# Hybrid decoder trunk on one core: each expert weight row stored as two halves of 4,096 bytes, 512 KB apart

## Chip, cores and metric

One core of a Trainium2 chip runs the kernel. The metric is the device time of one execution in microseconds, as the median of several runs. One more execution was profiled; all rows of the trace come from that one.

## What is computed

Two layers over 256 tokens of width 1024, all in float32. Each layer has a norm modulated by a conditioning vector, three parallel token mixers (a convolution module, a state-space module, an attention module), their gated merge, and then a feed-forward part. In layer 0 that is one dense SwiGLU of width 2816; in layer 1 it is eight experts of width 3584, of which each token uses two:

```python
def _swiglu(h, wg, wu, wd):
    return (jax.nn.silu(h @ wg) * (h @ wu)) @ wd

def _moe(h, router_w, router_b, wg, wu, wd):
    logits = (h @ router_w + router_b).astype(jnp.float32)
    top_v, top_i = lax.top_k(logits, MOE_TOPK)
    ...
    for e in range(N_EXPERTS):
        out = out + gates[..., e:e + 1] * _swiglu(h, wg[e], wu[e], wd[e])
    return out
```

A final norm follows. The weights of all eight experts are read in full: 8 x 3 x 1024 x 3584 values, 352 MB of the 531 MB that the kernel reads.

## The kernel before

**Work and stages.** Every large weight is cut on the host into units of 1 MB, stored so that one unit is a contiguous block of 128 rows (one for each partition of SBUF) of 2,048 float32 values, 8,192 bytes. The kernel goes through the stages in order: conditioning products, the input projection of layer 0, its mixers, its merge and its dense feed-forward part, then the same for layer 1 with the router and the experts at the end. Until the experts, SP loads units into a ring of six slots (L461 to L465), and POOL loads the units of the conditioning matrix (L544).

**The experts.** An expert has 42 units (`UNITS`, L48): for each of seven column groups of its hidden width two units of the gate matrix, two of the up matrix and two of the down matrix (`expert_units`, L83). They go in this order through 14 slots (`EXP_SLOTS`, L49; `eslot`, L180), which are pieces of several tensors: `aring`, `extra`, `ring`, `proj`, `xc`, `misc` and `sq`. So loads of `in_moe_units` stand in the trace under all these names. Unit u of an expert goes into slot u % 14.

**Who waits for whom.** `expert_load` (L467) is the one place that loads them; each load raises the semaphore `efull` of its slot by 16. PE waits for it in `arrived` (in `expert`), multiplies with the unit, and raises `unit_s` once for each unit that it is done with. SP runs a loop over the experts (L491 to L498): before it loads a unit it waits until the unit 14 places earlier is done with (L494, L497), so at most 14 units are ahead of PE. The first 14 loads of the first expert (L472 to L486) wait for the slots' earlier users, the last expert has a loop of its own (L500). Then SP stores the output in four DMAs of 128 rows of 2,048 bytes (L505 to L508); the destination's rows are 4,096 bytes apart.

**Order and sizes.** The experts are taken in an order that is found at run time (`turn`), and the matmuls of each are chosen by its number of tokens, rounded up to one of six sizes (`SIZES`, L46). For 32 tokens (`quarter_rows`, whose lines are L1046, L1065 and L1076) PE is done with a unit fastest. L984 and L1019 are the gate and up products and the down products where tokens are stationary, L1108 and L1124 those of large experts. At the end of each expert `prepare` turns a matrix (L1154) and gathers the next expert's tokens (L939). Each size is its own block of code, to which PE jumps at a change of expert (`expert_loop`, L421).

**On the host** `kernel` (L1974) puts the units of the experts together with `moe_layout` (L1938), in the shape expert, unit, row, 2048 (L1986).

Of the kernel before, what the change touches and what calls it, by code (L numbers as in the profile page):

```python
# [17 lines left out]
P = 128  # L18
# [12 lines left out]
FFN_DENSE, FFN_EXPERT, EXPERTS = 2816, 3584, 8  # L31
# [16 lines left out]
UNITS = 6 * GE  # L48
EXP_SLOTS = 14  # L49
# [44 lines left out]
def trunk(nc, x_cols, c_cols, par_cols, ada_units, dense_units, moe_units, out):  # L94
    fp32, i32 = mybir.dt.float32, mybir.dt.int32
    ALU, ACT, AX = mybir.AluOpType, mybir.ActivationFunctionType, mybir.AxisListType
    ds = bass.ds
# [4 lines left out]
    with ctx:  # L102
# [49 lines left out]
        for name, n in COLUMNS:  # L152
# [27 lines left out]
        eslot = ([aring[:, i, :] for i in range(ADA_SLOTS)] + [extra[:, :]]  # L180
                 + [ring[:, i, :] for i in range(SLOTS)]
                 + [proj[:, 48:56, :].rearrange("p a n -> p (a n)"), proj[:, 56:64, :].rearrange("p a n -> p (a n)"),
                    xc[:, 0:8, :].rearrange("p a n -> p (a n)"), misc[:, :], sq[:, :, :].rearrange("p a n -> p (a n)")])
# [155 lines left out]
        def released(key):  # L339

            kind, l, a = key
            if kind == "w":
                return proj_s, W_CHUNKS * l + a + 1
            if kind == "conf":
                return om_s, 16 * l + 2 * a + 2
            if kind == "attn":
                return om_s, 16 * l + 4 + 2 * a + 2
            if kind == "ssm":
                return om_s, 16 * l + 8 + a + 1
            if kind == "mix":  # L350
                return om_s, 16 * l + 12 + a + 1
            if kind in "gu":
                return gu_s, 2 * a + 2
            return dn_s, DN0 + a + 1
# [99 lines left out]
        @block.sync  # L454
        def _(sp):
            for i, a in enumerate(ADA_ORDER):
                sp.dma_start(ada_first[i], ada_units[a]).then_inc(afirst[i], 16)
                if i == 1:
                    sp.dma_start(xT[:, :, :], x_cols.rearrange("p (k n) -> p k n", k=KT)).then_inc(x_in_s, 16)

            for i, key in enumerate(ORDER):  # L461
                slot, _, before = PLAN[key]
                if before is not None:
                    sp.wait_ge(*released(before))
                sp.dma_start(ring[:, slot, :], dense_units[i]).then_inc(full[slot], 16)  # L465

            def expert_load(expert, u):  # L467

                sp.dma_start(eslot[u % EXP_SLOTS], moe_units[ds(expert, 1), u].rearrange("e p n -> p (e n)")  # L469
                             ).then_inc(efull[u % EXP_SLOTS], 16)  # L470

            for u in range(EXP_SLOTS):  # L472
                if u < ADA_SLOTS:
                    sp.wait_ge(apool_s, DEPTH * ADA_CHUNKS - ADA_FIRST)
                elif 3 <= u < 3 + SLOTS:
                    sp.wait_ge(*released(LAST[u - 3]))
                elif u in (9, 10):
                    sp.wait_ge(mg_s, 16 + 12)
                elif u == 11:
                    sp.wait_ge(gn_s, DEPTH)  # L480
                elif u == 12:
                    sp.wait_ge(om_s, 16 + 4)
                    sp.wait_ge(pv_s, HEADS_A * DEPTH)
                elif u == 13:
                    sp.wait_ge(h_s, 4 * KT)
                expert_load(0, u)  # L486
            def expert_of(place):
                return sp.value_load(turn[0:1, place], min_val=0, max_val=EXPERTS - 1)

            sp.wait_ge(ord_s, 1)  # L490
            with sp.Fori(0, EXPERTS - 1) as e:  # L491
                now, following = expert_of(ds(e, 1)), expert_of(ds(e + 1, 1))
                for u in range(EXP_SLOTS, UNITS):
                    sp.wait_ge(unit_s, e * UNITS + (u - EXP_SLOTS + 1))  # L494
                    expert_load(now, u)
                for u in range(EXP_SLOTS):
                    sp.wait_ge(unit_s, e * UNITS + (UNITS + u - EXP_SLOTS + 1))  # L497
                    expert_load(following, u)  # L498
            final = expert_of(slice(EXPERTS - 1, EXPERTS))
            for u in range(EXP_SLOTS, UNITS):  # L500
                sp.wait_ge(unit_s, (EXPERTS - 1) * UNITS + u - EXP_SLOTS + 1)
                expert_load(final, u)


            for q in range(2 * TT):  # L505
                sp.wait_ge(o_s, q + 1)
                t, cols = q % 2, slice((q // 2) * 512, (q // 2 + 1) * 512)
                sp.dma_start(out[0, t * P:(t + 1) * P, cols], o_tm[:, t, cols]).then_inc(od_s, 16)  # L508
            sp.wait_ge(od_s, 16 * 2 * TT)
# [1488 lines left out]
```

## Time and profile before

| | |
|---|---|
| median of 3 runs | 2032.22 us (2031.87 to 2032.5) |
| the profiled execution's own time | 2033.62 us |
| its span, first to last instruction | 2031.9 us |
| mean granted TensorE clock | 0.955 of full speed |
| PE busy (matmul / weight load) | 1887.1 us (93%) / 1326.6 us (65%) |
| DVE, ACT, POOL busy | 512.2, 279.6, 351.9 us |
| read from HBM | 531.08 MB, 262 GB/s over the span |
| expert loads | 336, of 1,024 KB each |

The profile shows one execution. Busy times are sums over the span, and a matmul's end is modelled, so a busy PE isn't PE at its peak. PE is matmuls and PEld weight loads; SPq is the queue in which SP issues DMAs. "DMA share" is the mean busy share of 16 DMA engines; the records of neighbouring packets overlap a little, so that it can be 1.01 or 1.02. The chain is the work that ended last, followed back from the end at each step to what released it. "issue" is time in which the engine waited for nothing that the profile shows.

### The profile page before, as it was taken

Reading aid. Unit: us, or ns where it says so; the run is one execution under the profiler, and the core shown is the slowest. Engines: PE = TensorE matmul, PEld = TensorE weight load, DVE = VectorE, ACT = ScalarE, POOL = GpSimd, SP = SyncE. Lnnn points to the kernel's source line nnn. Section 1 sums busy time; section 2 is a strip of 40 time slices with the busy share of each in tenths; the row PEclk is TensorE's granted clock in tenths of the full one; section 3 lists DMA queues with packets and bytes.
Section 4 is the critical chain, followed back from the end, with each engine's and each line's share of the span. In section 5 each row is a group of like instructions: output and inputs, shape, how many; then the busy total and the mean of one; then the engine's idle time right before and its main releaser. Section 6 shows DMA issues by size and latency. Waiting matters only on the chain.

```text
span 2031.9 us, 27702 instructions
## 1 busy us (share of the span) xinstructions
PE 1887.1 (93%) x11037; PEld 1326.6 (65%) x11038; DVE 512.2 (25%) x1144; ACT 279.6 (14%) x517; POOL 351.9 (17%) x215
## 2 busy tenths in 40 slices
PE   7999799989999999999977899998899979989796
PEld 5888588867776788888852688743444435555443
DVE  1794734110001292424141100011100110001112
ACT  2204212010000302422020000010000100010002
POOL 2609900079994000000000000000000000000000
PEclk8999899989999999999979899998999979999898
DMA  9645533257673444333459965589988899979993
GB/s 382 251 163 213 181 125 125 78 216 285 249 273 136 153 161 147 104 113 116 168 220 421 418 261 214 226 338 421 420 333 295 348 420 420 410 305 422 419 420 145
DMA packets 73857, 534.06 MB, mean 263 GB/s; under 512 B 8320, under 2 KB 8320, under 8 KB 8960
## 3 DMA queue, kind: packets, MB, share of 16 engines
q1 hardware_dynamic: 67680, 489.72, 61.6%
q0 software_dynamic: 5760, 41.95, 5.7%
q8 instruction: 103, 1.69, 0.3%
q10 hardware_dynamic: 288, 0.50, 0.1%
q14 instruction: 26, 0.21, 0.0%
HBM read 531.08 MB, written 1.05 MB: 262 GB/s over the span
## 4 chain that ended last, share of the span: by engine, by line
PE 83%; DMA 6%; DVE 4%; issue 3%; SPq 2%; ACT 2%; POOL 1%; DVEq 0%; ACTq 0%
PE ps L641 21%; PE ps L984 13%; PE ps L704 8%; PE ps L713 7%; PE ps L1019 6%; PE ps L1108 6%; PE ps L724 4%; PE ps L1124 3%; DMA xc<-in_moe_units 3%; DMA ring<-in_moe_units 3%; PE ps L1046 2%; PE ps L939 2%; SPq L469 2%; PE ps L1065 1%; PE ps L1076 1%
## 5 line engine op out<-in xcount | busy, mean ns | idle before, releaser
L641 PE MATMUL ps<-hT,ring 128*128 128x256 f32 x2048 | 455.4, 383 | 5.0 <-ACT hT L1236 5.0
L641 PEld LDWEIGHTS ps<-hT,ring 128*128 128x128 f32 x2048 | 390.6, 192 | 62.3 <-issue 8.3
L560 POOL TENSOR_TENSOR aring<-aring,ccol 128x2048 f32<-128x2048 f32 x40 | 145.0, 3624 | 234.5 <-ACT hT L1236 160.7
L713 PE MATMUL ps<-hT,ring 128*128 128x256 f32 x704 | 158.8, 388 | 4.0 <-ACT hT L1236 4.0
L713 PEld LDWEIGHTS ps<-hT,ring 128*128 128x128 f32 x704 | 136.5, 195 | 23.5 <-issue 4.4
L566 POOL TENSOR_TENSOR aring<-aring 128x1024 f32<-128x1024 f32 x80 | 149.5, 1869 | 6.3
L984 PE MATMUL ps<-ring,proj 128*64 128x256 f32 (+2 forms) x1144 | 131.2, 361 | 1.3 <-DMA ring<-in_moe_units 1.3
L1824 DVE TENSOR_TENSOR proj<-proj,ps 128x256 f32<-128x256 f32 (+2 forms) x28 | 14.6, 521 | 401.3 <-PE ps L984 401.3
L984 PEld LDWEIGHTS ps<-ring,proj 128*64 128x64 f32 (+2 forms) x1144 | 74.5, 132 | 52.4 <-issue 31.8
L1590 DVE SCALAR_TENSOR_TENSOR misc<-cpad,par,misc 128x256 f32<-128x256 f32 x240 | 102.7, 508 | 0.0
L704 PE MATMUL ps<-proj,ring 128*128 128x256 f32 x384 | 83.4, 379 | 0.0
L1241 ACT ACTIVATE proj<-ps 128x512 f32<-128x512 f32 x64 | 38.2, 596 | 328.5 <-PE ps L641 328.5
L704 PEld LDWEIGHTS ps<-proj,ring 128*128 128x128 f32 x384 | 72.8, 190 | 9.9
L724 PE MATMUL ps<-ring,proj 128*128 128x512 f32 x176 | 77.3, 592 | 0.0
L984 PE MATMUL ps<-aring,proj 128*64 128x256 f32 (+2 forms) x352 | 49.7, 420 | 27.8 <-issue 27.8
L1359 ACT ACTIVATE proj<-ps 128x256 f32<-128x256 f32 (+2 forms) x28 | 13.0, 464 | 380.9 <-PE ps L984 380.9
L1703 DVE TENSOR_TENSOR proj<-proj,ps 128x256 f32<-128x256 f32 x22 | 9.3, 421 | 211.9 <-ACT proj L1339 211.9
L1065 PEld LDWEIGHTS ps<-stk,proj 128*128 128x128 f32 x336 | 46.7, 222 | 23.7 <-issue 23.7
L984 PEld LDWEIGHTS ps<-aring,proj 128*64 128x64 f32 (+2 forms) x352 | 27.2, 154 | 51.9 <-issue 48.3
L1108 PE MATMUL ps<-proj,ring 128*128 128x160 f32 x416 | 60.0, 300 | 0.0
L704 PE MATMUL ps<-hT,ring 128*128 128x256 f32 x256 | 55.8, 380 | 3.0 <-DVE hT L1667 3.0
L1108 PEld LDWEIGHTS ps<-proj,ring 128*128 128x128 f32 x416 | 57.5, 190 | 0.8 <-issue 0.8
(345 smaller groups left out, 2117.7 us busy)
## 6 DMA issues: line engine op xcount, KB each, us to landing
ring<-in_moe_units SPq DMA_DIRECT2D x144, 1024.0 KB, 15.7
ring<-in_dense_units SPq DMA_DIRECT2D x121, 1024.0 KB, 5.0
aring<-in_moe_units SPq DMA_DIRECT2D x48, 1024.0 KB, 13.5
proj<-in_moe_units SPq DMA_DIRECT2D x48, 1024.0 KB, 18.1
aring<-in_ada_units POOLq DMA_DIRECT2D x40, 1024.0 KB, 6.0
extra<-in_moe_units SPq DMA_DIRECT2D x24, 1024.0 KB, 13.6
xc<-in_moe_units SPq DMA_DIRECT2D x24, 1024.0 KB, 20.1
misc<-in_moe_units SPq DMA_DIRECT2D x24, 1024.0 KB, 19.8
```

The source lines that it names most:

```text
L560: last = g.tensor_tensor(w, w, ccol[:, :].unsqueeze(2).broadcast_to([P, KT, 256]), ALU.mult)
L566: last = g.tensor_tensor(dst, w[:, 0:half_k, :], w[:, half_k:2 * half_k, :], ALU.add)
L641: last = mm(ps[:, n % 2, j * SEQ:(j + 1) * SEQ], wide(s)[:, k, j * P:(j + 1) * P], hT[:, k, :], start=(k == 0), stop=(k == KT - 1))
L704: last = mm(ps[:, idx % 2, j * SEQ:(j + 1) * SEQ], view(s)[:, k, (cols + j) * P:(cols + j + 1) * P], rhs[:, k, :], start=(k == 0), stop=(k ...
L713: last = mm(ps[:, j, c0:c0 + n], wide(w)[:, k, j * P:(j + 1) * P], x_src[:, k, 0:n], start=(k == 0), stop=(k == KT - 1))
L724: last = mm(dst, hm[:, b, j, t * P:t * P + rows], rows2(slot)[:, j, hf * 512:(hf + 1) * 512], start=(first and j == 0), stop=(stop and j = ...
L984: last = mm(ps[rows * c:rows * (c + 1), bank, 4 * t0:4 * (t0 + rows)], xg[:, 4 * h + k, t0:t0 + rows], w[:, k, 4 * rows * c:4 * rows * (c ...
L1019: last = mm(dst, hmt[:, g % 2, h0:h0 + rows], w[:, i, cols], start=(g == 0 and j == 0), stop=(g == GE - 1 and j == 3))
L1065: last = mm(ps[:, 4 + g % 2, c0 + j * n:c0 + (j + 1) * n], part[:, g % 2, j * P:(j + 1) * P], stk[:, :], start=True, stop=True)
L1108: last = mm(ps[:, j % 2, c0:c0 + n], w[:, k, j * P:(j + 1) * P], xg[:, 4 * h + k, 0:n], start=(h == 0 and k == 0), stop=(h == 1 and k == 3))
L1124: last = mm(dst, hmx[:, g % 2, j, t0:t0 + rows], w[:, i, cols], start=(g == 0 and j == 0), stop=(g == GE - 1 and j == 3))
L1590: v.scalar_tensor_tensor(cacc[:, m, :], cpad[:, m, ds(k, SEQ)], cwcol[:, l, ds(k * CT + m, 1)], cacc[:, m, :], ALU.mult, ALU.add).then_inc ...
```

## The change

Each unit of the experts is stored as two blocks of 128 rows of 1,024 values (4,096 bytes): the first halves of all rows, 512 KB, then the second halves. The load reads, for each partition, one piece from each block, and writes them side by side into the slot, so that the slot holds the same values at the same places. Each load then has 256 pieces of 4,096 bytes in place of 128 of 8,192. Number, order, size and waits of the loads are the same, and so are all other instructions.

```diff
             def expert_load(expert, u):
 
-                sp.dma_start(eslot[u % EXP_SLOTS], moe_units[ds(expert, 1), u].rearrange("e p n -> p (e n)")
+                sp.dma_start(eslot[u % EXP_SLOTS].rearrange("p (h n) -> p h n", h=2),
+                             moe_units[ds(expert, 1), u].rearrange("e h p n -> p (e h) n")
                              ).then_inc(efull[u % EXP_SLOTS], 16)
...
     t["moe_units"] = np.stack(moe_layout(inputs["moe_w_gate"][0], inputs["moe_w_up"][0], inputs["moe_w_down"][0])
-                              ).reshape(EXPERTS, UNITS, P, 2048)
+                              ).reshape(EXPERTS, UNITS, P, 2, 1024).swapaxes(2, 3)
```

## Rows read from the trace of the kernel before

**Rows 1.** The page: span, GB/s in 40 slices, chain by engine.

```profile
span 2031.9 us, 27702 instructions
...
GB/s 382 251 163 213 181 125 125 78 216 285 249 273 136 153 161 147 104 113 116 168 220 421 418 261 214 226 338 421 420 333 295 348 420 420 410 305 422 419 420 145
...
PE 83%; DMA 6%; DVE 4%; issue 3%; SPq 2%; ACT 2%; POOL 1%; DVEq 0%; ACTq 0%
```

**Rows 2.** The chain in order of time, expert stage: start us, us, what.

```profile
1092.60 26.79 DMA ring<-in_moe_units
...
1148.00 38.07 PE ps L1108 x256
...
1195.97 17.58 PE ps L1108 x128
...
1390.68 26.82 DMA xc<-in_moe_units
...
1625.08 26.85 DMA ring<-in_moe_units
...
1966.27 27.43 DMA xc<-in_moe_units
```

**Rows 3.** Busy time by windows of the expert stage; the first line names the columns.

```profile
core 0: us, PE busy (x) PEld busy (x) DVE busy (x) ACT busy (x) POOL busy (x), PEclk, DMA share, GB/s
1060.00:1070.00 10.00, 7.12 (x36) 4.39 (x36) 2.50 (x7) 1.35 (x2) 0.00 (x0) 0.66 0.80 318
1070.00:1120.00 50.00, 38.64 (x298) 14.02 (x300) 7.35 (x17) 3.50 (x8) 0.00 (x0) 0.93 1.01 421
...
1350.00:1420.00 70.00, 61.71 (x437) 28.13 (x430) 10.44 (x21) 7.14 (x15) 0.00 (x0) 0.90 1.01 421
...
1600.00:1660.00 60.00, 49.95 (x336) 20.74 (x339) 8.12 (x18) 4.37 (x10) 0.00 (x0) 0.85 1.01 422
...
1800.00:1810.00 10.00, 8.60 (x69) 4.22 (x68) 2.88 (x10) 1.31 (x3) 0.00 (x0) 1.00 0.64 242
1810.00:1820.00 10.00, 5.41 (x26) 3.15 (x28) 0.00 (x0) 2.65 (x5) 0.00 (x0) 0.66 0.36 117
...
1900.00:1990.00 90.00, 77.43 (x566) 41.00 (x564) 7.16 (x18) 6.82 (x15) 0.00 (x0) 0.92 1.01 420
...
2028.40:2030.90 2.50, 0.00 (x0) 0.00 (x0) 0.00 (x0) 0.40 (x1) 0.00 (x0) 1.00 1.03 385
```

**Rows 4.** Timeline of PE and PEld: start, us, instruction, in brackets idle before and releaser.

```profile
1129.37 0.14 PEld L1076 LDWEIGHTS ps<-xc,proj 128*32 128x32 f32 x4 [0.91 <-DMA xc<-in_moe_units]
...
1981.42 1.95 PE L984 MATMUL ps<-ring,proj 128*64 128x256 f32 x16 [0.63 <-DMA ring<-in_moe_units]
...
1993.74 0.20 PEld L1019 LDWEIGHTS ps<-xc,proj 128*64 128x64 f32 x4 [1.31 <-DMA xc<-in_moe_units]
```

**Rows 5.** The page: all DMA packets, and SP's queue (packets, MB, share of 16 engines).

```profile
DMA packets 73857, 534.06 MB, mean 263 GB/s; under 512 B 8320, under 2 KB 8320, under 8 KB 8960
...
q1 hardware_dynamic: 67680, 489.72, 61.6%
```

**Rows 6.** DMA queues in windows: q1 in 1070 to 1110, q10 in 13 to 18.

```profile
q1 hardware_dynamic: 2314, 16.79, 100.8%
...
q10 hardware_dynamic: 144, 0.49, 24.6%
```

**Rows 7.** SP's DMA instructions: expert loads into extra (ns min/median/max), and the output stores.

```profile
L469 SPq DMA_DIRECT2D extra<-in_moe_units x24: 332/333/1947, 979.8 to 1948.5; - x24
...
2027.38 1.82 SPq L508 DMA_DIRECT2D out<-proj  x4
```

**Rows 8.** Timeline of PE, first matmuls of an expert, with the idle time before.

```profile
1148.00 2.23 PE L1108 MATMUL ps<-proj,aring 128*128 128x160 f32 x7 [5.65 <-issue]
...
1814.59 1.98 PE L984 MATMUL ps<-aring,proj 128*64 128x256 f32 x8 [6.00 <-issue]
...
1913.76 6.15 PE L984 MATMUL ps<-aring,proj 128*64 128x256 f32 x32 [10.78 <-issue]
```

## Prediction

> **What bounds the kernel now.** I read the page first: the 40 slices show the DMA engines moving about 420 GB/s in several groups of slices of the second half, and mostly far below that before it [rows 1]. The first half can't be touched by a change of the expert loads alone; the question is what those groups cost. The shares of the chain say little (PE 83%, DMA 6%), since they are a mean over stages [rows 1]. So I followed the chain in order of time through the expert stage. It goes through a landing of expert weights four times: landings at 1119.4, 1417.5, 1651.95 and 1993.7, each 27 us after its issue [rows 2]. Between these the chain is PE alone. The experts differ in size: the first, third and fifth (32 token columns) use a unit faster than it can be loaded, the second and fourth are slow on PE and let the loads run 14 units ahead again. Rows by windows give the length of each full stretch [rows 3]:
>
> - A: the queue fills at about 1062 (share 0.80 in 1060 to 1070) and is full until the last wait on the chain at 1119.4: 57 us
> - B: 1350 to 1417.5: 67 us
> - C: 1600 to 1652: 52 us
> - D: after the loads had caught up (shares 0.64 and 0.36 in 1800 to 1820), from about 1830 to 1993.7: 164 us
>
> Together 340 us, all at 420 to 422 GB/s. The waits at the end of D are real though small: 0.63 us for one unit at 1981.4, and 1.31 before the weight load at 1993.74 [rows 4], so nothing of a later landing is hidden there. In A a wait of 0.91 us is seen as late as 1129.4 [rows 4], so A could count as 67 us rather than 57, and C likewise as 62; I keep that for the range (360 us).
>
> **What the change does to the packets.** The page has 73,857 packets, 67,680 on SP's queue; 466 loads and 4 stores make that 144 each, 128 rows and 16 completion packets [rows 5]. The 336 expert loads get 128 more each: 336 x 128 = 43,008, so 116,865 packets, with the same 531 MB. No instruction is added to an engine; SP issues as many DMAs as before, and the first 14 loads (before 1060) come while the DMA engines have idle time, so they cost nothing (the cover is PE's work to 1050).
>
> **The price of a packet.** Two stretches of the trace have the DMA engines full with packets of one size: expert loads of 8,192 bytes at 421 GB/s, and the output stores of 2,048 bytes at 385 GB/s [rows 3]. For one of 16 engines that is 8192 x 16 / 421 = 311.3 ns and 2048 x 16 / 385 = 85.1 ns a packet. The line through both has 0.0368 ns a byte and 9.7 ns for each packet. Eight more packets per engine and load would be 8 x 9.7 = 78 ns; as a part of the 9.7 ns (an eighth of a completion packet) is not doubled, I take 70 ns. A load goes from 1.0486 MB / 421 = 2.491 us to 2.56, 2.8% more, at about 410 GB/s.
>
> The bounds. Above: loads from 3,840-byte rows took 24.6% of 16 x 5 us = 19.7 us for 128 rows and 16 completions, so at most 154 ns a row, where 8,192 bytes took 100.8% of 640 us over 2,314 packets, of which 264 are completions, so at most 315 ns [rows 6]. A row of 4,096 would be 154 + 256 x 0.0368 = 163.4 ns, two of them 326.8, 12 ns over 315: 94 ns a load, 3.8%. Below: nothing, if the fixed part of a packet is hidden behind the data of the one before, and the stores' lower rate is due to their being stores. Not below nothing: no row has a rate above 422 GB/s. I take 70, since it comes from spacing and not from the length of records, which overlap (they sum to a share of 1.01). The Trainium skill (DMA: Bandwidth & Descriptors, section iDMA fabric) has one SP load stream of 1 MiB per DMA with 4 KiB rows at 408.7 GB/s; by that the load would take 2.566 us, an extra 75 ns, and the sum below 10.2 us. No run here shows that figure yet.
>
> **Sum.** 340 us / 2.491 = 136 loads on the path, 136 x 0.070 = 9.6 us: A 1.6, B 1.9, C 1.5, D 4.6. The terms add up: where a stretch ends in a wait, all that PE does later moves by its term, and the next full stretch starts later by as much. Between C and D the loads fall behind by 80 x 0.07 = 5.6 us from 1600 to 1800, of which PE's own shift takes 1.5; the 10 us in which the DMA engines stood idle between 1800 and 1820 cover the other 4.1 [rows 3]. If that cover were gone, D would begin at 1600.
>
> Against the profiled execution (2033.6 us, span 2031.9) this gives 2043.2. The median of the runs is 2032.2, so 1.4 lower: **2041.8 us**, 0.5% slower.
>
> **SP and its queue.** An expert load that finds room is issued in 0.33 us, the median; in the full stretches SP is often held for about 1.9 us or more, the most for this slot 1.95 [rows 7]. If the limit is in packets, a load with 256 rows fills twice the room, about 5 loads are on their way instead of 27 / 2.49 = 11, and time from issue to landing falls towards 14 us, while SP is held for the rest. Behind the held SP are only further expert loads, in the order in which they are wanted, and 5 loads still are 13 us of work, so this costs nothing. Making 128 rows into packets isn't what takes the 1.9 us: four stores of 128 rows were issued within 1.82 us [rows 7] and ran at 385 GB/s, that is 0.68 us for each, so 256 rows need at most 1.4 us, under the 2.56.
>
> **PE's clock.** The waits of A pull the granted clock to 0.93 [rows 3], and the next expert's first piece takes 38.07 us for 256 matmuls where 2 x 17.58 is usual, 2.9 us more [rows 2]. Waits that get longer can move such a drop; I add nothing and allow 3 us either way.
>
> **Rivals.**
> - *The fixed part is hidden* (12 in 100). The price is 0 to 30 ns a load, 0 to 4 us: 2032 to 2036. For it: the two sizes in the line differ in direction as well. Against: 3,840-byte loads lie near the same line. The same page of the Trainium skill (section Why small descriptors are slow) counts some 3 bus cycles a packet, 259 against 2 x 131: 1.2%, by which the sum would be 4.0 us. The trace's line is above that.
> - *Faster, by instruction fetches* (3 in 100). At changes of expert PE stands idle for code: 5.65 us at 1142, 10.78 at 1903, and twice 5.5 between, all with full DMA engines [rows 8]. If those fetches wait behind queued packets and half the packet means half the wait, 13.7 us come back against 9.6 lost: 2028.1. It decides once more than 9.6 us come back. Against: 6.00 us at 1808 [rows 8], while the DMA engines had idle time [rows 3]. So the wait isn't the queue's.
> - *The rate falls by 10%* (5 in 100), as the two halves of a row lie 512 KB apart in HBM and their reads get in each other's way. From 0.17 us a load (59 x 0.17 = 10) the idle time at 1800 is used up and D begins at 1600: (340 + 178) / 2.49 = 208 loads, at 0.25 us each 52 us, less 10: 2074. No strided load is in the trace; the stores write half rows at a step of 4 KB and fit the line, which speaks against.
> - *SP's queue becomes the bound* (2 in 100). If the 1.93 us were a price for 128 rows, 256 would take 4.1 us a load with its wait; 322 loads, 1320 us instead of the 934 from 1060 to 1994: 2420. The stores speak against it, as above.
>
> **Chances and range.** The forecast has 78 in 100; its own range is 40 to 94 ns over 340 to 360 us (5.5 to 13.7 us), with the clock's 3 us at the ends: 2035.5 to 2048.5. That leaves out most of the hidden case, the faster one and both large ones, about 20 in 100. A measurement of this kernel can tell 0.2%, 4.1 us, from no change. Faster 0.03; same 0.12; slower 0.78 + 0.05 + 0.02 = 0.85.
>
> **What the profile after would show.** Right: 116,865 packets, the same MB; full windows at 408 to 412 GB/s instead of 421; PE, DVE and ACT busy as before; the same four landings on the chain, later by about 1.6, 3.5, 5.0 and 9.6 us; idle DMA time left near 1810; landing after 14 or 27 us, by the queue's limit. Wrong: full windows still at 418 or more (hidden); shares of 1.0 without a break from 1600 to the end (D merged); shorter idle times for code at changes of expert (the faster rival); DMA shares well below 1 in the small experts (SP bound). If the rate is 410 but the time moves by less than 5 us, my count of loads on the path is the failed step.

## The result and the profile after

| | before | after |
|---|---|---|
| median (lowest to highest) | 2032.22 us (2030.8 to 2040.5, 5 runs) | 2043.09 us (2040.95 to 2046.09, 5 runs) |
| ratio, 95% interval | | 1.0050 (1.0035 to 1.0065) |
| profiled execution: its time / span | 2033.62 / 2031.9 us | 2045.66 / 2043.9 us |

The change makes the kernel 0.5% slower: 10.9 us by the medians, 10.2 (7 to 13) by the ratio. The two profiled executions are 12.0 us apart; that of after is 2.6 us above its median, and the places below add up to the 12.0.

The page of the changed kernel: span, GB/s in 40 slices, packets, SP's queue, chain by engine.

```profile
span 2043.9 us, 27702 instructions
...
GB/s 380 247 160 215 180 124 124 83 218 276 251 281 140 151 146 142 123 104 124 165 251 409 405 258 216 223 336 409 409 339 293 347 409 408 408 332 409 407 409 143
DMA packets 116865, 534.06 MB, mean 261 GB/s; under 512 B 8320, under 2 KB 8320, under 8 KB 94976
...
q1 hardware_dynamic: 110688, 489.72, 62.7%
...
PE 78%; DMA 7%; SPq 6%; DVE 3%; issue 3%; ACT 2%; POOL 1%; DVEq 0%; ACTq 0%
```

As many instructions and bytes as before and 43,008 packets more [rows 1, 5]. Every slice that stood at about 420 GB/s stands at about 409 now; most others hardly differ. The chain has moved 5% of the span from PE to SP's queue and the DMA engines. That doesn't make SP the bound: on the chain a load now takes 18 to 21 us from issue to landing and not 27, SP is held longer before it can issue one, and the DMA engines are full all the while, so the same wait for weights is followed back through SP for longer. The windows that answer to [rows 3]:

```profile
1070.00:1120.00 50.00, 38.80 (x284) 15.35 (x276) 6.27 (x14) 3.50 (x8) 0.00 (x0) 0.90 1.03 409
1130.00:1140.00 10.00, 9.29 (x40) 6.65 (x37) 1.11 (x4) 0.28 (x1) 0.00 (x0) 0.54 1.03 409
1370.00:1430.00 60.00, 50.96 (x328) 24.15 (x326) 8.32 (x19) 3.78 (x9) 0.00 (x0) 0.83 1.03 409
1600.00:1660.00 60.00, 51.72 (x355) 22.19 (x352) 8.97 (x19) 5.65 (x11) 0.00 (x0) 0.86 1.03 409
1810.00:1820.00 10.00, 5.15 (x46) 1.47 (x42) 1.13 (x4) 3.97 (x7) 0.00 (x0) 0.92 0.85 318
1820.00:1830.00 10.00, 8.72 (x64) 5.49 (x66) 0.00 (x0) 0.38 (x1) 0.00 (x0) 0.74 0.41 142
1900.00:1990.00 90.00, 75.35 (x538) 40.48 (x538) 9.92 (x27) 6.44 (x14) 0.00 (x0) 0.94 1.03 408
```

A load takes 1.0486 MB / 409 = 2.564 us where it took 2.491: 73 ns more, 9.1 ns for each of the 8 added packets of an engine. The idle time of the DMA engines between stretches C and D is still there, near 1820 (0.85 and 0.41). The chain in order of time, and first matmuls of three experts (PE timeline), which answer to [rows 2] and [rows 8]:

```profile
1110.40 20.69 DMA xc<-in_moe_units
...
1368.97 18.58 DMA xc<-in_moe_units
...
1405.02 18.33 DMA xc<-in_moe_units
...
1649.12 20.77 DMA xc<-in_moe_units
...
1958.67 18.39 DMA aring<-in_moe_units
...
1986.50 18.81 DMA xc<-in_moe_units
```

```profile
1152.47 2.76 PE L1109 MATMUL ps<-proj,aring 128*128 128x160 f32 x9 [5.54 <-issue]
1821.28 1.98 PE L985 MATMUL ps<-aring,proj 128*64 128x256 f32 x8 [6.13 <-issue]
1919.72 1.55 PE L985 MATMUL ps<-aring,proj 128*64 128x256 f32 x6 [10.70 <-issue]
```

The same four stretches end in a landing, now all in `xc`, the 40th unit of an expert; in A and C that unit is four later than the one on the chain before, and B and D have one more landing inside them. Against the rows before, PE is 4.5 us late at the start of the second expert (1152.47 for 1148.00), 6.7 at the seventh (1821.28 for 1814.59), 6.0 at the eighth, and 12.0 at the end. By the starts of all eight experts, the four that hold the stretches got longer by 4.5 (A), 3.1 (B), 1.3 (C) and 6.0 us (D), 14.9 together, and the four that PE bounds got shorter by 0.6 to 0.9 each, 2.9 together. The first piece of the second expert shows this; it took 38.07 us before [rows 2], and now, in two parts, 37.08:

```profile
1152.47 5.20 PE ps L1109 x23
1157.74 31.81 PE ps L1109 x233
```

The idle times for code at a change of expert are as before (5.54, 6.13, 10.70 for 5.65, 6.00, 10.78).

### The profile page after: what moved, and what is told of

Read it like the earlier page. It is cut to its first block, busy times and chain, and to the rows that moved or that the text cites. A ratio compares the mean times of both kernels' runs of the same rounds, so it can differ in the third digit from the quotient of the medians.

```text
span 2043.9 us, 27702 instructions
## 1 busy us (share of the span) xinstructions
PE 1890.1 (92%) x11037; PEld 1329.5 (65%) x11038; DVE 507.0 (25%) x1144; ACT 279.7 (14%) x517; POOL 351.6 (17%) x215
## 3 DMA queue, kind: packets, MB, share of 16 engines
HBM read 531.08 MB, written 1.05 MB: 260 GB/s over the span
## 4 chain that ended last, share of the span: by engine, by line
PE 78%; DMA 7%; SPq 6%; DVE 3%; issue 3%; ACT 2%; POOL 1%; DVEq 0%; ACTq 0%
PE ps L642 21%; PE ps L985 12%; PE ps L705 7%; PE ps L714 7%; PE ps L1109 6%; PE ps L1020 6%; SPq L469 6%; DMA xc<-in_moe_units 5%; PE ps L725 4%; PE ps L1125 3%; PE ps L940 2%; PE ps L1047 1%; DMA proj<-in_ada_units 1%; DMA aring<-in_moe_units 1%; PE ps L1077 1%
## 5 line engine op out<-in xcount | busy, mean ns | idle before, releaser
L1825 DVE TENSOR_TENSOR proj<-proj,ps 128x256 f32<-128x256 f32 (+2 forms) x28 | 14.6, 521 | 404.7 <-PE ps L985 404.7
L1066 PEld LDWEIGHTS ps<-stk,proj 128*128 128x128 f32 x336 | 48.6, 230 | 24.7 <-issue 24.7
## 6 DMA issues: line engine op xcount, KB each, us to landing
ring<-in_moe_units SPq DMA_DIRECT2D x144, 1024.0 KB, 17.6
```

## The experiments

My theory: each packet has a fixed price, some 9 ns of its DMA engine, and the kernel pays it only on the 136 or so loads that lie in full stretches which end in a wait. Rivals: the distance between the halves in HBM; the DMA of 256 rows itself (SP's issue, the room in its queue); a price that all 336 loads pay alike. Each ratio is to runs of the kernel before made beside it, whose medians lay from 2033.1 to 2034.6 us, and losses in microseconds are worked out from the ratio; so a time alone isn't to be compared with the 2032.22 above.

### Packet or distance: halves side by side in HBM

```diff
-                             moe_units[ds(expert, 1), u].rearrange("e h p n -> p (e h) n")
+                             moe_units[ds(expert, 1), u][:, :, :, 0:1024].rearrange("e p h n -> p (e h) n")
...
-                              ).reshape(EXPERTS, UNITS, P, 2, 1024).swapaxes(2, 3)
+                              ).reshape(EXPERTS, UNITS, P, 2, 1024)
+    t["moe_units"] = np.concatenate([t["moe_units"], t["moe_units"][..., :64]], -1)
```

> The halves of each row stay beside each other in HBM, 256 bytes apart (rows of 2 x 1,088 values of which 1,024 are read), so each load has 256 packets of 4,096 bytes as in the changed kernel, but nothing is read 512 KB away. If the price belongs to the packet (my theory: some 8 to 9 ns each, 8 more for each engine and load): full windows at 408 to 410 GB/s as in the changed kernel, and 2041 to 2045 us, 10 to 11 above the kernel before. If it belongs to the distance between the halves: full windows back at 420 or 421 GB/s and 2032 to 2034 us.

Measured: 2044.91 us, ratio to before 1.0053 (1.0038 to 1.0067). Windows of this kernel, behind stretch A and in it:

```profile
1130.00:1140.00 10.00, 9.62 (x53) 7.17 (x54) 3.04 (x8) 0.28 (x1) 0.00 (x0) 0.92 1.03 410
1070.00:1120.00 50.00, 39.35 (x276) 15.34 (x268) 6.36 (x14) 3.50 (x8) 0.00 (x0) 0.86 1.03 409
```

The same rate, and the same loss within 0.2%, with the halves 256 bytes apart as with 512 KB. The distance costs nothing that can be measured here.

### More packets: quarters and eighths of a row

```diff
-                sp.dma_start(eslot[u % EXP_SLOTS].rearrange("p (h n) -> p h n", h=2),
+                sp.dma_start(eslot[u % EXP_SLOTS].rearrange("p (h n) -> p h n", h=4),
...
-                              ).reshape(EXPERTS, UNITS, P, 2, 1024).swapaxes(2, 3)
+                              ).reshape(EXPERTS, UNITS, P, 4, 512).swapaxes(2, 3)
```

For the eighths it is h=8 and (8, 256).

> Each row in four pieces of 2,048 bytes, 256 KB apart: 512 packets a load, 24 more for each engine than before. If each packet has a fixed price of 8.5 ns: 204 ns a load, 2.69 us in place of 2.49, full windows at about 389 GB/s (the output stores with packets of this size ran at 385). 136 loads on the path give 28 us; from 1600 to 1800 the loads fall 59 x 0.204 = 12 us further behind than PE's own shift covers, against 10 us of idle time, so the idle time near 1810 is gone and 2 us more are lost: 2062 us, range 2056 to 2070. If the price is one for reading a row in more than one place and not for each packet: 409 GB/s still and 2043 us. If SP is the bound for 512 rows (256 rows took 0.37 us when there was room): DMA shares below 1 in the small experts and over 2080.

> Each row in eight pieces of 1,024 bytes, 128 KB apart: 1,024 packets a load, 56 more for each engine. By a fixed 8.7 ns each: 0.49 us a load, 2.98 us, full windows at 352 GB/s. By the same count (A 24 and B 27 loads, then from 1600 to the end one full stretch of 148 loads less 10 us of idle time): 12 + 13 + 62 = 87 us, about 2120 us, range 2105 to 2135. If SP's making of packets is the bound for 1,024 rows in one instruction, the DMA share falls below 1 in the small experts, the rate is lower than 350, and the time over 2140.

Measured: quarters 2069.17 us, ratio 1.0172 (1.0157 to 1.0186), 35 us; eighths 2132.1 us (2 runs), ratio 1.0478 (1.0459 to 1.0498), 97 us. Windows of the quarters:

```profile
1070.00:1120.00 50.00, 38.21 (x264) 14.81 (x259) 6.36 (x14) 3.50 (x8) 0.00 (x0) 0.83 1.05 387
...
1800.00:1810.00 10.00, 10.00 (x143) 6.53 (x143) 0.00 (x0) 0.98 (x2) 0.00 (x0) 1.00 1.05 387
1810.00:1820.00 10.00, 9.93 (x132) 5.14 (x129) 1.27 (x3) 0.49 (x1) 0.00 (x0) 1.00 1.05 386
1820.00:1830.00 10.00, 9.40 (x76) 4.89 (x74) 3.17 (x11) 0.54 (x1) 0.00 (x0) 1.00 1.05 386
```

and of the eighths:

```profile
1640.00:1660.00 20.00, 14.58 (x98) 4.61 (x100) 2.57 (x6) 0.87 (x2) 0.00 (x0) 0.82 1.10 348
```

Two things are to be seen. The price is the same for each packet: loads of 2.710 us (387 GB/s) and 3.013 us (348) are 219 and 522 ns over 2.491, for 24 and 56 more packets of an engine: 9.1 and 9.3 ns each, as for 8. And the quarters have shares of 1.05 right through 1800 to 1830: the idle time that covered part of the loss is used up, C and D have become one stretch. With the measured prices the sums that the expectations used give 136 x 0.219 + 59 x 0.219 - 10 = 33 us for the quarters, and 51 x 0.522 + 148 x 0.522 - 10 = 94 for the eighths, beside 35 and 97 measured. SP isn't the bound even with 1,024 rows in a DMA, as the windows stay full.

### Which loads pay: the first 14 units or the other 28

The first kernel stores and loads only the first 14 units of each expert in halves, the second only the other 28. The load of the first kernel (the host stores these units to match, which isn't shown; the second has `u < EXP_SLOTS`):

```diff
+                if u >= EXP_SLOTS:
+                    sp.dma_start(eslot[u % EXP_SLOTS], moe_units[ds(expert, 1), u].rearrange("e p n -> p (e n)")
+                                 ).then_inc(efull[u % EXP_SLOTS], 16)
+                    return
+                sp.dma_start(eslot[u % EXP_SLOTS].rearrange("p (h n) -> p h n", h=2),
...
```

> Halves 512 KB apart only in the first 14 units of each expert (112 of 336 loads), the other 28 as before. By my count of the path only the last expert's 14 are on it (stretch D; in stretches A to C the path runs through units from 13 to 39 of the small experts, and the first 14 of the others are loaded in cover): 14 x 0.07 = 1.0 us, so 2033 to 2034 us, same as before by 0.2%. If all loads cost alike, as a mean rate would have it: a third of the 10.9 us, 2036 us.

> The other part of the change: the first 14 units of each expert as before, units 14 to 41 (224 of 336 loads) in halves. By my count 122 of the 136 loads on the path: 8.5 to 10 us, 2041 to 2042 us. If all loads cost alike: two thirds of 10.9 us, 7.3, 2039.5 us. This run and the one with the first 14 should add up to the whole change in either case; what tells the theories apart is their ratio, 9 to 1 or 2 to 1.

Measured: first 14: 2034.56 us, ratio 1.0004 (0.9993 to 1.0014), so 0.8 us and at most 2.8. Other 28: 2040.78 us, ratio 1.0037 (1.0023 to 1.0051), 7.5 us. The first kernel has a third of the added packets and about a tenth of the loss. A price that all loads pay alike would give it 3.6 us of the 10.9, which is outside the interval (by the lowest loss that the main comparison allows, 7.1 us, it would be 2.4, which is inside). The 7.5 us is lower than the 8.5 to 10 expected and its interval (4.7 to 10.4 us) holds both theories; it is the first of the two that tells. The two losses add up to 8.3 us, for 10.2 of the whole change, which the intervals allow. The trace shows the place too. Of the first kernel's profiled execution PE is 0.3 us late at the start of the second expert (1148.32), 0.2 at the eighth (1914.00), and 2.3 at the end (a span of 2034.2); its last landing on the chain comes 1.9 us later than before:

```profile
1968.12 27.48 DMA xc<-in_moe_units
```

So what it loses, it loses in D, as the count of the path has it, and the first units of the other experts cost at most a few tenths of a microsecond.

### Bigger packets: neighbouring units as rows of 16,384 bytes

```diff
+                if slot in PAIRS:
+                    sp.dma_start(wide_slot[slot], moe_units[ds(expert, 1), u:u + 2]
+                                 .rearrange("e two (q r) n -> e (two q) (r n)", r=2)
+                                 .rearrange("e p n -> p (e n)")).then_inc(efull[slot], 16)
+                    return
...
-                    sp.wait_ge(unit_s, e * UNITS + (u - EXP_SLOTS + 1))
+                    sp.wait_ge(unit_s, e * UNITS + (u + more - EXP_SLOTS + 1))
```

> The other direction: where two neighbouring slots lie side by side in SBUF (aring, the three pairs of ring, the two pieces of proj: 10 of 14 units), both units are loaded by one DMA of 128 rows of 16,384 bytes, stored side by side on the host. A pair is loaded once its second slot is free, and counts as landed as a whole. If the price is 8.5 to 9 ns for each packet, a pair saves 8 packets and a completion for each engine, some 75 ns: full windows go from 421 to about 426 GB/s, and 136 loads on the path give 5/7 x 136 x 0.037 = 3.6 us back. Against that each full stretch starts later by up to one unit of PE's work (1 to 2 us) and its wait can end later by as much, four times: net between 2 us faster and 6 us slower than before. If a packet's price isn't fixed but grows with its bytes beyond some size, the rate stays at 421.

Measured: 2036.35 us, ratio 1.0009 (0.9999 to 1.0019). Window and waits of PE in stretch A:

```profile
1070.00:1120.00 50.00, 38.77 (x276) 15.56 (x268) 6.36 (x14) 3.50 (x8) 0.00 (x0) 0.86 1.01 427
```

```profile
1086.12 1.06 PE L1091 MATMUL ps<-ring,proj 128*32 128x512 f32 x8 [1.27 <-DMA ring<-in_moe_units]
1091.02 1.94 PE L1061 MATMUL ps<-proj 128*32 128x512 f32 x8 [2.98 <-DMA proj<-in_moe_units]
```

The rate rises to 427 GB/s as it should, which is 35 ns a unit or 4.8 us over 136 loads, and the time doesn't fall: in stretch A PE waits up to 2.98 us for a pair, where the longest wait there was 1.52 us before. That the coarser landing and the later issue take what the packets give is the likely reading; no run parted the two. No kernel here beats the one before.

### Is it the DMA of 256 rows: two DMAs for each unit

```diff
-                sp.dma_start(eslot[u % EXP_SLOTS], moe_units[ds(expert, 1), u].rearrange("e p n -> p (e n)")
-                             ).then_inc(efull[u % EXP_SLOTS], 16)
+                for h in range(2):
+                    cols = slice(1024 * h, 1024 * (h + 1))
+                    sp.dma_start(eslot[u % EXP_SLOTS][:, cols],
+                                 moe_units[ds(expert, 1), u][:, :, cols].rearrange("e p n -> p (e n)")
+                                 ).then_inc(efull[u % EXP_SLOTS], 16)
```

> The stored layout of before, and each unit loaded by two DMAs of 128 rows of 4,096 bytes (first the first halves of all rows, then the second halves), each with its own 16 completions; PE waits for both. So the packets have the size of the changed kernel, but no single DMA has 256 rows, and nothing is 512 KB apart. If the price belongs to the packet: 16 packets and 2 completions for each engine and unit, 2.57 to 2.58 us a unit, 407 to 408 GB/s, and 2042 to 2046 us. If it belongs to a DMA of 256 rows (SP's making of the packets, or the room in its queue): 418 to 421 GB/s and 2032 to 2035 us. On the queue: with 128 rows a DMA the changed kernel's time from issue to landing (18 us median, at most 22, so 8 units on their way where there were 12) tells what the room is counted in. If in DMAs: 12 half units, at most 15 us. If in packets or bytes together, about 22 us again.

Measured: 2058.2 us, ratio 1.0122 (1.0102 to 1.0143). The full windows ran at 409 GB/s, so the rate belongs to the packets here too and not to a DMA of 256 rows. From issue to landing it took 17.6 us at most, some 14 half units, between the two numbers expected. But the time is 24.7 us up, and neither theory had that. Windows, and SP's instructions in order of time, of this kernel:

```profile
1350.00:1360.00 10.00, 10.00 (x80) 4.88 (x84) 2.58 (x5) 2.16 (x3) 0.00 (x0) 1.00 0.57 195
1600.00:1610.00 10.00, 10.00 (x85) 4.41 (x84) 1.62 (x4) 5.12 (x7) 0.00 (x0) 1.00 0.48 168
```

```profile
1600.73 0.87 SPq L471 DMA_DIRECT2D sq<-in_moe_units  x2
1609.21 2.52 SPq L471 DMA_DIRECT2D aring<-in_moe_units  x4
```

The load into `sq` is the last in SP's loop over the experts and that into `aring` the first of its next turn: SP does nothing from 1601.6 to 1609.2, at the very point where stretch C should start. PE isn't what it waits for: PE's first matmuls of the new expert, which free the slots in `aring`, began at 1600.17 and took 1.92 us. The kernel before has 2.0 us at each of these two turns. The next kernel writes that loop out flat:

```diff
-            with sp.Fori(0, EXPERTS - 1) as e:
-                now, following = expert_of(ds(e, 1)), expert_of(ds(e + 1, 1))
+            for e in range(EXPERTS - 1):
+                now = expert_of(slice(e, e + 1))
...
```

> The kernel with two DMAs a unit was 24.6 us slower, not 10, though its full windows ran at 409 GB/s. Its trace has SP idle for 6.6 us at 1347.2 and 7.6 us at 1601.6, where its loop over the experts turns back, and the DMA engines near half busy in those windows (0.57 and 0.48). Here SP's loop is written out flat, with the same loads, waits and packets. If the loop's turn (fetching the head of a loop whose code has become longer) made the rest of the loss: no such gaps, about 14 us less than with the loop, 2042 to 2046 us, ratio 1.004 to 1.006. If two DMAs a unit cost that time in another way (completions, SP's issues): it stays at 2055 to 2060 us.

Measured: 2049.17 us, ratio 1.0075 (1.0058 to 1.0093). In its trace SP goes from `sq` to `aring` within a microsecond, in the same two places:

```profile
1347.08 1.85 SPq L471 DMA_DIRECT2D sq<-in_moe_units  x2
1349.70 2.08 SPq L471 DMA_DIRECT2D aring<-in_moe_units  x4
...
1596.44 0.85 SPq L471 DMA_DIRECT2D sq<-in_moe_units  x2
1598.07 1.88 SPq L471 DMA_DIRECT2D aring<-in_moe_units  x4
```

Flat, the kernel is 9.6 us nearer to the one before (1.0122 to 1.0075), not the 14 expected, of some 14.6 that were too many beside the changed kernel. The other 5 stay open: 1.0075 and 1.0050 are for the same data packets, and their intervals overlap by little. It still has two completions and two issues for each unit; by the starts of PE's experts its C (with the expert behind it) is 3.9 us longer than in the changed kernel, D 2.2 and B 1.3, while its A is 2.7 shorter. No run parted these.

## Why the prediction was right

**Sign and size.** 2041.8 was forecast and 2043.09 measured, inside the forecast's own range; 9.6 us more were forecast and 10.9 measured (10.2, 7 to 13, by the ratio). The range put down, 2035.5 to 2048.5, isn't quite what its terms give (2032.2 + 5.5 - 3 = 2034.7 and 2032.2 + 13.7 + 3 = 2048.9); nothing hangs on it. That the sum came this near is in part luck, as its places show below.

**The price of a packet** was the main term, drawn from loads of 8,192 and stores of 2,048 bytes. 70 ns a load were taken and 73 measured; 410 GB/s forecast, 409 seen. The line of two points held for rows of 1,024 to 8,192 bytes, and the stores' rate (385) is that of loads with packets of their size (387), so direction was no matter. The bound from the 3,840-byte rows (94 ns) was too high; it rests on the lengths of records, which overlap the more the smaller the packets are (shares of 1.01, 1.03, 1.05 and 1.10 from 8,192 down to 1,024 bytes). The Trainium skill (DMA: Bandwidth & Descriptors, section iDMA fabric) gives 408.7 GB/s for loads of this form, and the trace agrees with 409. The 3 bus cycles a packet of its section Why small descriptors are slow would be 3 of the 259 of a row of 8,192 bytes, an estimate of 3.6 ns by the 311 ns of such a row here; the runs show 9.1 to 9.3, so the measurement decides against it.

**The loads on the path.** 136 were counted, 9.6 us. The runs with a part of the units bear the kind of count out (some loads pay, most don't), not each of its terms. By places the four stretches cost 14.9 us, 5 more than 136 loads at the measured 73 ns, and the experts that PE bounds gave 2.9 back, which no term had. The two misses work against each other; that much of the good sum is luck. (With the halves side by side it is 14.3 and 2.7. Each place is read from one execution, and those of one kernel differ by some microseconds, so the tenths don't count for much.)

The largest miss is A: 4.5 us where 1.6 was forecast. In the kernel before the 40th unit of the first expert is waited for until 1129.37 [rows 4]; in the changed kernel it lands at 1131.09. These 1.7 us are about what the price makes of the loads up to there (27 loads in 67 us, the longer of the two counts of A, at 73 ns: 2.0). The other 2.8 us lie behind that landing, in PE's clock. The kernel before, first, then the changed one with its chain:

```profile
1120.00:1130.00 10.00, 10.00 (x52) 4.66 (x48) 0.98 (x2) 0.87 (x2) 0.00 (x0) 0.50 1.01 420
1130.00:1140.00 10.00, 10.00 (x61) 7.92 (x54) 3.49 (x9) 0.28 (x1) 0.00 (x0) 0.98 1.01 422
```

```profile
1131.13 1.93 PE ps L1077 x8
1133.07 3.55 PE ps L1066 x16
```

In both kernels the granted clock drops to about half of full speed after PE has waited for unit after unit. Before, it falls in 1120 to 1130, where PE still has a unit to wait for, and is over soon after it has landed (0.98 in 1130 to 1140). In the changed kernel it falls in 1130 to 1140 (0.54), when nothing is left to wait for and every slow matmul counts. With the halves side by side, the same packets, the drop is missing there and comes in B:

```profile
1130.38 1.69 PE ps L1077 x8
1132.07 1.90 PE ps L1066 x16
...
1419.52 1.93 PE ps L1077 x8
1421.46 3.55 PE ps L1066 x16
```

16 matmuls take 1.90 us at a granted clock of 0.92 (1130 to 1140 of that kernel), and 3.55 at 0.54. From the landing in A to the next expert's start it is 18.4 us there and 21.3 in the changed kernel; from that in B 19.0 us there and 16.3 in the changed kernel. So the place of the drop moves 3 us from one stretch to another, and both kernels end 12 us late (11.6 and 12.0). The 3 us allowed for the clock were the right size for one place; between these two kernels they make no difference at the end.

B cost 3.1 for 1.9 forecast, C 1.3 for 1.5, D 6.0 for 4.6. D was counted from 1830 on, but the DMA engines of the kernel before are full again sooner, so it holds a few more loads than the 66 of the sum:

```profile
1820.00:1830.00 10.00, 10.00 (x92) 6.44 (x90) 0.42 (x1) 1.13 (x3) 0.00 (x0) 1.00 0.97 386
```

The price of 73 for 70 ns and these loads make about 0.5 us; the other 0.9 of D, and what B has too much, no run parted. The landings that were to be later by 1.6, 3.5, 5.0 and 9.6 us came later by 1.7 in A (the same unit), 5.9 in B and 11.6 in D; in C the one on the chain is another unit.

**What was covered.** The first 14 units cost next to nothing outside D, and the experts that PE bounds nothing, as said; the idle time of the DMA engines near 1810 covered C's lag (their idle time in 1800 to 1830 fell from some 10 us to some 7, by the shares), and at the quarters' 0.22 us a load it is used up, above the 0.17 worked out as the point; that point itself was not tried.

**The rivals.** The hidden fixed part fell with 409 GB/s. The faster one fell with unchanged idle times for code. That reading across 512 KB slows the loads fell with the halves side by side. SP as the bound fell with full windows at 1,024 rows.

**The queue was half right.** Time from issue to landing was to be 14 or 27 us, by whether room is counted in packets or loads. It was at most 21.7, which fits neither (see below). That it costs nothing held: SP's issue took 0.37 us for 0.33 [rows 7], and no window of a full stretch shows less than full DMA engines.

## What to carry to other kernels

A row that is cut in two costs each DMA engine one more fixed price, here 9 ns beside 311 for 8,192 bytes, whatever the distance of the pieces; find it by comparing two windows of the kernel's own trace in which the DMA engines are full, with packets of different size. Multiply it not by all loads but by those in full stretches that end in a wait, and then ask how much idle DMA time is left between two such stretches, since the loss grows faster once it is gone, as in the quarters. Add up by place as well as in all: a sum can be right because two misses cancel. Bigger packets raised the rate here and the time didn't fall.

## What the runs showed that I had not expected

- **Room in SP's queue.** The longest time from issue to landing was 30.0 us with 128 rows a load, 21.7 with 256, 17.0 with 512 and 13.4 with 1,024. Divided by the time of a load that is 12, 8.5, 6.3 and 4.4 loads on their way: neither a fixed number of loads nor one of packets. What it is counted in stays open.
- **A loop's turn on SP.** With two DMAs for each unit in place of one, in the same loop, SP stood idle for 6.6 and 7.6 us where the loop turned back; with the loop written flat these gaps were gone. The small instruction queue (q14) moved 59 packets in that kernel, 26 in the changed one and 40 with the loop written flat. That the code's length is what does it was not tried by itself.
